# A decoder step with grouped experts: expert results scattered to token order and reloaded in line, down weights as row pairs, third expert's weights behind the first gathers

## What is computed

```python
g_sel = argmax(xt @ router_group)                       # 1 of 4 groups
top_p, top_i = top_k(softmax(le_sel), 2)                # 2 of its 8 experts
for e in range(32):
    hdn = silu(xt @ w_gate[e]) * (xt @ w_up[e])         # 1024 -> 256
    y = y + comb[:, e:e + 1] * (hdn @ w_down[e])        # 256 -> 1024
out = rmsnorm(h + y, norm_final)                        # h: residual stream
```

## Time and profile before

| | us |
|---|---|
| median of 3 runs (range) | 1054.51 (1053.08 to 1056.87) |
| the profiled execution | 1052.6 |
| its span, first to last instruction | 1050.8 |
| PE busy, all of it | 909.5 (87%) |
| DVE busy | 607.8 (58%) |
| ACT busy | 500.9 (48%) |
| POOL busy | 235.7 (22%) |
| first gather issued | 675.3 |
| first transposes of block 0 | 683.2 |
| copy of the last block's result begins | 992.8 |
| last norm begins | 1046.4 |

### The profile page before, as it was taken

How to read it: one execution, slowest core, us unless ns; L and a number is a source line. 1 busy time by engine, 2 the same in 40 slices (tenths; PEclk the granted TensorE clock), 3 DMA queues, 4 the chain that set the end, 5 groups by cost and what they waited for, 6 DMA issues and landing times. The chain is left out here.

```text
span 1050.8 us, 14271 instructions
## 1 busy us (share of the span) xinstructions
PE 909.5 (87%) x4955; PEld 716.5 (68%) x4955; DVE 607.8 (58%) x1037; ACT 500.9 (48%) x861; POOL 235.7 (22%) x300
## 2 busy tenths in 40 slices
PE   4899999999999999958969999499999999999700
PEld 3799887887788778835658665377777777777400
DVE  4504432352326332757555326778999899889457
ACT  4523434334433434344312111558888888888312
POOL 1102322222322322323222211211011110100075
PEclk9999999999999999979989998689999999999955
DMA  8123123222131113270253433989999999999685
GB/s 258 39 84 96 63 71 91 75 86 72 57 108 54 46 33 102 76 252 11 57 179 120 155 106 124 359 321 387 388 395 390 393 387 386 394 397 355 250 288 200
DMA packets 90859, 202.33 MB, mean 193 GB/s; under 512 B 11839, under 2 KB 53631, under 8 KB 82598
## 3 DMA queue, kind: packets, MB, share of 16 engines
q1 hardware_dynamic: 80302, 168.40, 45.1%
q0 software_dynamic: 5984, 17.18, 4.8%
q10 hardware_dynamic: 4504, 15.85, 4.0%
HBM read 167.00 MB, written 38.41 MB: 195 GB/s over the span
## 5 line engine op out<-in xcount | busy, mean ns | idle before, releaser
L993 PE MATMUL pj<-n_hi,w_hi 128*128 128x350 f32 (+1 forms) x576 | 198.5, 345 | 3.6 <-DVE n_lo L1313 3.6
L993 PE MATMUL pj<-n_lo,w_hi 128*128 128x350 f32 (+1 forms) x576 | 188.3, 327 | 0.0
L993 PE MATMUL pj<-n_hi,w_lo 128*128 128x350 f32 (+1 forms) x576 | 187.5, 325 | 0.0
L1896 DVE TENSOR_TENSOR e_lo<-e_raw,e_hig 128x2048 fp32r<-128x2048 f32 x64 | 145.9, 2282 | 0.0
L993 PEld LDWEIGHTS pj<-n_hi,w_hi 128*128 128x128 f32 x576 | 109.4, 190 | 32.4 <-issue 30.6
L1275 DVE CUSTOM_DVE_ANT_0 sc<-pj,strip 128x512 f32<-128x512 f32 (+5 forms) x120 | 61.0, 544 | 118.9 <-PE pj L1059 77.4
L1892 ACT ACTIVATE e_hig<-e_raw 128x2048 fp32r<-128x2048 f32 x64 | 122.5, 1918 | 8.0 <-DMA e_raw<-in_w_up 7.6
L993 PEld LDWEIGHTS pj<-n_lo,w_hi 128*128 128x128 f32 x576 | 109.8, 191 | 0.6
L993 PEld LDWEIGHTS pj<-n_hi,w_lo 128*128 128x128 f32 x576 | 109.7, 190 | 0.7 <-issue 0.6
L1944 PE MATMUL pj<-e_hig,xT_hi 128*96 128x512 f32 x256 | 105.3, 411 | 0.0
L1944 PE MATMUL pj<-e_hig,xT_lo 128*96 128x512 f32 x256 | 101.8, 398 | 0.0
(11 more groups left out here) (267 smaller groups left out, 1629.1 us busy)
## 6 DMA issues: line engine op xcount, KB each, us to landing
e_raw<-in_w_up SPq DMA_DIRECT2D x32, 1024.0 KB, 15.2
e_raw<-in_w_gate SPq DMA_DIRECT2D x32, 1024.0 KB, 17.7
e_raw<-in_w_down SPq DMA_DIRECT2D x32, 1024.0 KB, 19.8
w_raw<-in_w_in SPq DMA_DIRECT2D x24, 512.0 KB, 4.1
expert_rows<-yo ACTq DMA_DIRECT2D x32, 384.0 KB, 7.9
expert_rows<-logits SPq DMA_DIRECT2D x22, 384.0 KB, 4.6
wo_raw<-in_w_out SPq DMA_DIRECT2D x8, 512.0 KB, 5.0
k_page<-in_cache_k SPq DMA_DIRECT2D x16, 256.0 KB, 3.8
```

Source lines behind the costliest of these rows:

```text
L993: ins = pe.matmul(pj[g % 2][:, 0:tn], ws[w][:, P * k:P * (k + 1)], x[:, k, t0:t0 + tn], start=(m == 0), stop=(m == 23))
L1896: eng.tensor_tensor(e_lo[r][:, q, :], e_raw[r][:, q, :], e_hi(par, q).bitcast(F32), ALU.subtract).then_inc(s_lo[q], 1)
```

## The change

1. **Scatter.** `expert_rows` is now in token order, rows 2t and 2t+1 for the two results of token t. POOL writes a block's rows there by an indirect DMA (`scatter`) in place of ACT's plain store. The route constants carry 2t+1 and 2t+2, the list is kept as `slot_row`, and `slot_tok` comes from it by one more DVE operation, a shift. `addr` and the zero writes go. In POOL's order gather n+5 stands ahead of scatter n.
2. **Linear reload.** SP reloads each token tile's pairs of rows with one plain DMA of 8 KB a partition, nine DMAs in all, into nine buffers `f_y`. Result tiles are made in place in `f_h`.
3. **Final part on two engines.** For five of the nine tiles (`BY_PE`: 1, 2, 4, 5, 7) PE sums residual and first row in a PSUM bank, as `ident @ f_h` and `diag(gate) @ f_y`, four float32 matmuls of 512 columns; DVE adds the second row, in two halves. DVE makes the five diagonals. The norm of a tile comes two tiles later, not one. The residual tiles 6, 7, 8 and the last gain are loaded after block 28, the others after block 29.
4. **Overflow.** The test `extra > 0` stands around the loop of 22 passes.
5. **Down weights.** Partition p gets the rows 2p and 2p+1 of w_down, 8 KB in one piece, where it got rows p and p+128, 4 KB each. So the two transposes of the hidden tile `hh` read every second column.
6. **Third expert.** Its three loads also wait for the first two gathers (and for the last logits), as the fourth's did.

```diff
     hn_dram = dram("normed", (TOK, D))
-    y_dram = dram("expert_rows", (CB * MAXB, D))
...
-                if 1 <= s <= XB:
-                    if s == 1:
-                        sp.wait_ge(s_lam, 3)
-                    sp.dma_start(y_dram.rearrange("(p b) (q c) -> p b q c", b=MAXB, c=256)[:, NE + s - 1:NE + s].rearrange("p a q c -> p (a q) c"),
-                                 bass.AP(tensor=zero_row.tensor, offset=zero_row.offset, ap=[[zero_row.ap[0][0], CB], [0, 4], [1, 256]])).then_inc(s_fill, 16)
...
-            do(dve.tensor_scalar(slot_f[0:CB, :], pj[1][0:CB, 0:NE], 0.0, 4096.0, ALU.is_equal, ALU.mult))
+            do(dve.tensor_scalar(slot_f[0:CB, :], pj[1][0:CB, 0:NE], 0.0, 8192.0, ALU.is_equal, ALU.mult))
             do(dve.scalar_tensor_tensor(slot_f[0:CB, :], pj[1][0:CB, 0:NE], -1.0, slot_f[0:CB, :], ALU.add, ALU.add))
-            do(dve.tensor_copy(slot_tok[0:CB, 0:NE], slot_f[0:CB, :]))
+            do(dve.tensor_copy(slot_row[0:CB, 0:NE], slot_f[0:CB, :]))
+            do(dve.tensor_scalar(slot_tok[0:CB, 0:NE], slot_row[0:CB, 0:NE], 1, None, ALU.arith_shift_right))
             dve.sem_inc(s_slots, 1)
...
-                src = w[bass.ds(expert, 1)].rearrange("a (f p) c -> p (a f) c", p=P)
-                dst = e_raw[r][:, q, :].rearrange("p (f c) -> p f c", f=2)
+                src = w[bass.ds(expert, 1)].rearrange("a (p f) c -> p (a f c)", p=P)
+                dst = e_raw[r][:, q, :]
...
+        def scatter_from(pool, index, par):
+            pool.indirect_dma_start(y_dram, bass.IndirectOffsetOnAxis(ap=index, axis=0), yo[0:CB, par, :], None,
+                                    bounds_check=2 * TOK - 1, oob_is_err=False).then_inc(s_yst[par], 16)
+
+        def scatter(pool, n, par):
+            pool.wait_ge(s_y0, n + 1)
+            pool.wait_ge(s_y1, n + 1)
+            scatter_from(pool, slot_row[0:CB, n:n + 1], par)
...
+            units = hh[0:CB, :].rearrange("s (p f) -> s f p", f=2)
             for f in range(2):
-                ins = pe.transpose(ht_bank[:, CB * f:CB * (f + 1)], hh[0:CB, P * f:P * (f + 1)], C("ident")[0:CB, 0:CB])
+                ins = pe.transpose(ht_bank[:, CB * f:CB * (f + 1)], units[:, f, :], C("ident")[0:CB, 0:CB])
...
-            with eng.Fori(0, XB) as x:
-                with eng.If(x < extra):
+            with eng.If(extra > 0):
+                with eng.Fori(0, XB) as x:
                     body(NE + x, RD - 1, 1, x)
 
         def sp_m(sp):
             sp.wait_ge(s_dm, 2 * NT)
-            for q in (1, 0, 2):
-                load_piece(sp, 2, q, 2, 0, 2)
             sp.wait_ge(s_lge, NT)
             sp.wait_ge(s_hsq, NT)
             for r in range(2):
                 sp.wait_ge(s_xg[r], 16)
-            for q in (1, 0, 2):
-                load_piece(sp, 3, q, 3, 0, 3)
+            for e in (2, 3):
+                for q in (1, 0, 2):
+                    load_piece(sp, e, q, e, 0, e)
...
-            sp.sem_inc(s_ally, 1)
+            sp.wait_ge(s_more, 1)
+            for i in range(NT):
+                sp.dma_start(f_y[i][0:ROWS[i], :, :], y_dram[2 * P * i:2 * P * i + 2 * ROWS[i]].rearrange("(t c) d -> t c d", c=2)).then_inc(s_fy[i], 16)
+                if i == 0:
+                    sp.sem_inc(s_ally, 1)
 
...
-            for n in range(3):
-                gather(pool, n, n)
+            for n in range(5):
+                gather(pool, n, n % RD)
             for n in range(NE):
-                if n + 3 < NE:
-                    gather(pool, n + 3, (n + 3) % RD)
+                if n + 5 < NE:
+                    gather(pool, n + 5, (n + 5) % RD)
+                scatter(pool, n, n % 2)
...
-                if 0 <= n - 2:
-                    store_block(act, n - 2, n % 2)
...
-        f_y = at("f_y", [P, RF, 2, D], F32, r0 + 24576)
-        f_o = at("f_o", [P, RF, D], F32, r0 + 57344)
+        f_y = [at(f"f_y{i}", [P, 2, D], F32, r0 + 24576 + 8192 * i if i < 6 else r_o + 8192 * (i - 6)) for i in range(NT)]
...
+        BY_PE = [i for i in range(NT) if i not in (0, 3, 6, NT - 1)]
...
         def final_loads(sp):
 
+            sp.wait_ge(s_dn, NE - 3)
             sp.dma_start(g_fin[:], bass.AP(tensor=I["norm_final"].tensor, offset=0, ap=[[0, P], [1, D]])).then_inc(s_dconst, 16)
-            for i in range(NT):
+            for i in (6, 7, 8, 0, 1, 2, 3, 4, 5):
+                if i == 0:
+                    sp.wait_ge(s_dn, NE - 2)
                 sp.dma_start(f_h[i][0:ROWS[i], :], h_dram[cols(i)]).then_inc(s_fh[i % RF], 16)
...
+            for i in BY_PE:
+                M = ROWS[i]
+                dve.tensor_scalar(f_diag[0:M, i, :], C("ident", M), gate_w[0:M, 0, i:i + 1], None, ALU.mult).then_inc(s_fdiag, 1)
...
+                if i in BY_PE:
+                    n = BY_PE.index(i)
+                    dve.wait_ge(s_fy[i], FY)
+                    dve.wait_ge(s_fsum, 3 + n + 1)
+                    for b in range(2):
+                        part = slice(512 * b, 512 * (b + 1))
+                        dve.scalar_tensor_tensor(f_h[i][0:M, part], f_y[i][0:M, 1, part], gate_w[0:M, 1, i:i + 1], f_bank[n % 4][b][0:M, :],
+                                                 ALU.mult, ALU.add).then_inc(s_fs, 1)
+                else:
+                    dve.wait_ge(s_fh[r], FH0 + 16 * len(range(r, NT, RF)))
+                    dve.wait_ge(s_fy[i], FY)
+                    for c in range(2):
+                        dve.scalar_tensor_tensor(f_h[i][0:M, :], f_y[i][0:M, c, :], gate_w[0:M, c, i:i + 1], f_h[i][0:M, :],
+                                                 ALU.mult, ALU.add).then_inc(s_fs, 1)
+                        if c == 0:
+                            dve.wait_ge(s_fs, 2 * i + 1)
+                if i >= LR:
+                    norm(i - LR)
+            for i in range(NT - LR, NT):
+                norm(i)
+
+        def pe_f(pe):
+            pe.wait_ge(s_ally, 1)
+            for i in range(RF):
+                pe.wait_ge(s_fh[i], FH0 + 16 * len(range(i, NT, RF)))
+
+            def residual(n):
+                M = ROWS[BY_PE[n]]
+                if n >= 4:
+                    pe.wait_ge(s_fs, 2 * BY_PE[n - 4] + 2)
+                for b in range(2):
+                    pe.matmul(f_bank[n % 4][b][0:M, :], C("ident", M)[:, 0:M], f_h[BY_PE[n]][0:M, 512 * b:512 * (b + 1)], start=True, stop=False)
+
+            for n in range(2):
+                residual(n)
+            for n, i in enumerate(BY_PE):
+                M = ROWS[i]
+                pe.wait_ge(s_fdiag, 1 + n + 1)
+                pe.wait_ge(s_fy[i], FY)
+                for b in range(2):
+                    ins = pe.matmul(f_bank[n % 4][b][0:M, :], f_diag[0:M, i, 0:M], f_y[i][0:M, 0, 512 * b:512 * (b + 1)], start=False, stop=True)
+                ins.then_inc(s_fsum, 1)
+                if n + 2 < len(BY_PE):
+                    residual(n + 2)
```

97 lines of the change are left out of this document (40 added, 57 removed).

## The result

| | before | after |
|---|---|---|
| median of the runs, us | 1053.8 (1050.9 to 1057.0, 8 runs) | 1060.0 (1056.6 to 1061.4, 8 runs) |
| ratio, 95 % interval | | 1.0056 (1.0039 to 1.0072) |
| span of the profiled execution, us | 1050.8 | 1057.2 |
| first transposes of block 0 | 683.2 | 678.8 |
| last block's `yo` copy begins | 992.8 | 1009.6 |

The account below looks back on a forecast made before the run. PE was taken to bound the block loop, with DMA also busy and its backlog growing; no engine was full in the final part. Terms -11.7 + 2.5 - 2 + 0.5 = -10.7 gave a median of 1043.8 us, range 1038 to 1051.

Parts of the forecast that it names:

- Term 1: Final part: scatter, linear reloads and residuals on PE end the span at 1039.1, -11.7 us; ends -13 and -4.7.
- Term 2: Block loop: the third expert's later load adds backlog, partly offset by the scatter's fewer bytes; +2.5 us, between 0 and 6.
- Its first part: Block loop: the later load leaves 6.5 us of lasting backlog, 26.3 us in the 880s against a 22 us threshold.
- The rival that let it bind in full: Block loop: uneven DMA engines, no early gain; +6 instead of +2.5, 0 instead of -2, 1049.3 us; chance 0.20.
- Its sign: Late in the loop: w_up landing at over 22 us and blocks over 9.5 us apart would show the backlog binds.
- Its second part: Block loop: the scatter moves 0.268 MB a block, the store 0.393; saving from 0 to 6.4 us over 20 blocks.
- the slow-scatter rival: Block loop: scatters landing later than 17.4 us delay `y_half`; at 19 us, +24, about 1068 us; chance 0.07.
- Term 3: Start of the loop: first gather lands in about 6 us instead of 8, -2 us; ends 0 and -3.7.
- My 1 us: Start of the loop: by packet turns between queues, weights delay the first gather's 96 packets by no more than about 1 us.
- Small ones: Strided hidden transposes cost +0.5 us, ends 0 and 3.8; removed DMA issues, POOL's scatters and zero writes cost nothing.
- The chances: Whole kernel: faster 0.86, same 0.06, slower 0.08; the forecast with both terms about as worked out 0.57.

Follow-up runs that it names:

- x1: After, with the third expert's three loads back in their old place, ahead of the wait on the first two gathers: 1053.2 us, ratio to before 0.9993.
- x9: Before, with only the third expert's loads held back behind the first two gathers: 1058.3 us, ratio to before 1.0035.
- x2: After, with w_down loaded as rows p and p+128 again and plain hidden transposes: 1061.3 us, ratio to before 1.0064.
- x3: After, with both the third expert's loads early and w_down as rows p and p+128: 1053.3 us, ratio to before 0.9991.
- x10: x5 with its plain block store issued by GpSimd behind the gather instead of by ScalarE, for timing alone: 1052.8 us, ratio to before 0.9994.
- x5: x3 with ScalarE's plain store of each block to 96 adjacent rows in place of the scatter, for timing alone: 1042.0 us, ratio to before 0.9867.
- x4: Before, with only w_down loaded as adjacent row pairs (8 KB per partition) and strided hidden transposes: 1052.0 us, ratio to before 0.9988.
- x6: x3 with the scatter's index replaced by 96 adjacent rows, for timing alone: 1051.4 us, ratio to before 0.9960.
- x7: Before, with its plain block store issued by GpSimd behind the gather instead of by ScalarE: 1092.4 us, ratio to before 1.0346.
- x12: Before, with gathers replaced by plain loads of 72 fixed rows per block on ScalarE's queue, for timing alone: 1065.1 us, ratio to before 1.0096.
- x13: x3 with gathers replaced by plain loads of 72 fixed rows on ScalarE's queue, scatter left on GpSimd's, for timing alone: 1050.0 us, ratio 0.9957.

## Why the prediction was wrong

- **What bounds the kernel.** Right: PE without a gap, DMA full beside it, and a backlog that grows. I took the rate of 389 GB/s for a constant of the machine. It belonged to the way in which the streams lay on the queues.
- **Term 1, final part, -11.7: measured -10.4.** The scatter and SP's start took 5.6 us from the copy of `yo` where I had 6.4, the first tile's load 5.0 where I had 4.8, PE's four residuals 5.1 where I priced half clock at 7.0 (the clock of that stretch was 0.74). First add to the end of the last norm: 32.4, worked out 32.0. The empty passes went as expected: DVE's 16.71 us without a shown wait became 1.15. What fell short is the tail behind the last norm: 4.5 us instead of 3.1.
- **Term 2, the loop: +2.5 forecast, +21.2 measured.** This is the failed step, in both of its parts.
- **Its first part, the third expert's later load: measured +10.7 for this edit** (x1) and 10.0 by itself (x9); net of the earlier start x9 costs 0.35 % of the time, about 4 us. I had one cost, a backlog that had to pass 22 us at the last blocks, and let saved bytes pull it under again. There were two. In the first block the loads themselves were late: I had the third's w_up landing 5 us after its issue and not waited for, and never asked about the fourth's, which now stands behind the third's three loads. They landed after 9.8 and 19.1 us, and the first block took 2.8 to 4.4 us longer (x2 against x3, x9 against before, after against x1). The rest, 5.9 us in x9, is the lasting backlog. The rival that let it bind in full had that mechanism, and at +6 about the size of this part; it had nothing for the first block. Its sign came as named: w_up landed after over 22 us from the 730s on, and the blocks stood over 9.5 us apart.
- **Its second part, the scatter: 0 or better forecast, by bytes saved; measured +10.5** (x1 against before; x10 against x5). I bounded the scatter's effect on the DMA by zero on the bad side. That the store's move to the gathers' queue could slow the weights was in neither the sum nor a rival: the slow-scatter rival asked only when scatters land, and they landed after 7.8 us, under the 17.4 from which it decides.
- **How the two add up.** Before's own landings of w_up rise to 21.7 us at 900 without a wait of PE, so it has next to no slack left for either part: 10.0 (x9) and 10.5 (x1) alone, 21.2 together. x1's blocks keep 9.4 us up to 814 and take 10.4 from there to 971 (15 blocks); after's, whose w_up lands after 17 to 23 us from the 680s to the 740s, take 10.36 already from 761 on.
- **Term 3, start, -2: measured -4.4**, 3.3 of it in the landing of the first gather. The other 1.1 is when that gather was issued, and it isn't the change's: in the kernels that gather, profiled once each, it lay between 674.2 and 677.4. The landing is clear: 4.5 to 4.7 us without the third expert's loads ahead of it (after, x2, x9), 7.0 to 8.6 with them. My 1 us from the rule of the Trainium skill ("DMA: Bandwidth & Descriptors", "Queues, rings and completion order") is too small. It counted a packet of the rule as one packet of the profile, while the section has an engine drain a whole packet of typically 9 to 17 descriptors before it switches; so it is my estimate that failed, and no run here decides on the rule. The start was worth less than it cost.
- **Small ones.** Down weights in pairs and strided transposes: nothing that x2, x3 and x4 could tell from zero, as I had it, and far from the 3.8 of the upper end. The 2.02 us that I read for each gather of results beside a busy DVE is the first of each pair; the second took 0.95. It was not in the sum.
- The chances. 0.86 on faster rested on a range of 0 to +6 for everything that the loop could do short of late scatters. The loop did +21.2.

What stays open is why reads of rows beside the weights lower the rate of all queues, and whether it is the shared queue itself or the order and time of reads and writes on it that lengthens them. Every kernel with reads of rows and stores on one queue was slow (after, x1 to x3, x6, x7, x10 to x12), but x13 was slow with the two apart, and its plain loads of fixed rows differ from gathers in more than their queue.

## What to carry to other kernels

Where a loop is short of DMA time, a stage's GB/s is not a price to multiply bytes with: ask of each change which streams will share a queue, above all with the row reads, and what that did elsewhere. Work that is moved from an idle stretch into such a loop can cost its full length, however much slack the first iterations show (here 8 us of DMA work, and 10 us of loop in the executions profiled); ask also which loads stand behind it on their queue. And changes that touch different stages want measuring one at a time: here the final part alone was worth 0.9 %, and the two loop edits around it lost that and more.
